# Four branch results turned by VectorE and device memory instead of by TensorE

## The reference

```
h = x @ w_in                                   # 2048 -> 18688 columns, split
y_a = pool_mixer(a_in, ...)      * silu(a_gate)     # each y: 256 tokens x 1024
y_b = spatial_gating(u, v, ...)  * silu(b_gate)
y_c = sliding_window_attention(q, k, v, ...) * silu(c_gate)
y_d = conformer_conv(d_in, ...)  * silu(d_gate)
gates = sigmoid(g_logits)                      # 4 x 2048 columns
merged = sum_i gates[i] * (y_i @ w_branch[i])  # 1024 -> 2048
out = merged @ w_out
x = layer_norm(ALPHA * x + out)
```

## Time and profile before

| | |
|---|---|
| median of three runs | 2425.29 us (2425.19 to 2425.72) |
| profiled execution | 2426.32 us, its span 2424.6 us |
| PE (matmul) busy | 2402.5 us, 99% |
| weight loads of PE busy | 1977.9 us, 82% |
| DVE busy | 1800.6 us, 74% |
| ACT busy | 1119.0 us, 46% |
| POOL busy | 162.2 us, 7% |
| TensorE clock granted | 0.999 of full |
| moved by DMA | 556.93 MB, mean 230 GB/s |

### The profile page before, as it was taken

The page is one execution under the profiler, slowest core; times in us unless marked ns, Lnnn a source line. Parts: engine busy times, 40 slices in busy tenths (PEclk is TensorE's granted clock), DMA queues, the critical chain, the costliest instruction groups (busy, mean ns, idle before and its releaser), DMA issues.

```text
span 2424.6 us, 28710 instructions
## 1 busy us (share of the span) xinstructions
PE 2402.5 (99%) x11098; PEld 1977.9 (82%) x11098; DVE 1800.6 (74%) x2429; ACT 1119.0 (46%) x1464; POOL 162.2 (7%) x186
## 2 busy tenths in 40 slices
PE   9999999999999999999999999999999999999998
PEld 7888888888888888888788888777788888888887
DVE  5688868888899888788878857677777765555555
ACT  5344444444455454456743333644544443444443
POOL 2010000000000001000011100002000100000000
PEclk9999999999999999999999999999999999999999
DMA  9888766666588668877985656455898976667663
GB/s 303 256 269 273 239 218 195 195 184 195 188 267 267 211 213 292 293 257 255 316 270 186 222 171 233 132 159 177 268 302 283 292 233 193 195 211 227 210 213 124
DMA packets 280100, 556.93 MB, mean 230 GB/s; under 512 B 18503, under 2 KB 23901, under 8 KB 278428
## 3 DMA queue, kind: packets, MB, share of 16 engines
q1 hardware_dynamic: 270588, 515.16, 66.0%
q0 software_dynamic: 9088, 37.85, 5.4%
q10 hardware_dynamic: 288, 2.10, 0.2%
HBM read 543.07 MB, written 15.11 MB: 230 GB/s over the span
## 4 chain that ended last, share of the span: by engine, by line
PE 94%; DVE 3%; issue 1%; ACT 1%; DMA 1%; SPq 0%; POOL 0%; ACTq 0%; POOLq 0%; DVEq 0%
PE pb L2155 92%; PE pb L2159 3%; DVE wlo L1395 1%; DMA raw<-in_w_in 1%; DVE acc L1417 1%; ACT whi L939 0%; DVE sm L1946 0%; DVE x L1774 0%; DVE across L1427 0%; DVE gn L2015 0%; DVE x L1777 0%; DVE x L1495 0%; DVE stz L1497 0%; DVE x L1510 0%; DVE fl L2003 0%
## 5 line engine op out<-in xcount | busy, mean ns | idle before, releaser
L939 ACT ACTIVATE whi<-raw 128x1024 fp32r<-128x1024 f32 (+1 forms) x791 | 828.2, 1049 | 1105.5 <-PE pb L2155 1030.5
L1395 DVE TENSOR_TENSOR wlo<-raw,whi 128x1024 fp32r<-128x1024 f32 (+1 forms) x791 | 958.1, 1218 | 446.8 <-ACT whi L939 444.6
L2155 PE MATMUL pb<-whi,xh 128*128 128x512 f32 (+1 forms) x1184 | 465.1, 393 | 0.7 <-DVE xl L1548 0.7
L2155 PE MATMUL pb<-whi,xl 128*128 128x512 f32 (+1 forms) x1184 | 458.2, 387 | 0.0
L2155 PE MATMUL pb<-wlo,xh 128*128 128x512 f32 (+1 forms) x1184 | 457.6, 386 | 0.0
L1417 DVE SCALAR_TENSOR_TENSOR acc<-raw,silc,acc 128x512 f32<-128x512 f32 x480 | 346.1, 752 | 5.7 <-DMA raw<-in_w_ada 0.7
L2155 PE MATMUL pb<-whi,fh 128*128 128x512 f32 x704 | 274.8, 390 | 1.4 <-DVE fl L2003 1.4
L2155 PE MATMUL pb<-whi,fl 128*128 128x512 f32 x704 | 274.0, 389 | 0.0
L2155 PE MATMUL pb<-wlo,fh 128*128 128x512 f32 x704 | 273.9, 389 | 0.0
L2155 PEld LDWEIGHTS pb<-whi,xh 128*128 128x128 f32 x1184 | 222.6, 188 | 46.6 <-issue 2.9
L2155 PEld LDWEIGHTS pb<-whi,xl 128*128 128x128 f32 x1184 | 222.3, 188 | 46.0
(11 more groups left out here) (426 smaller groups left out, 2828.9 us busy)
## 6 DMA issues: line engine op xcount, KB each, us to landing
raw<-in_w_in SPq DMA_DIRECT2D x375, 512.0 KB, 4.6
raw<-in_w_ada SPq DMA_DIRECT2D x192, 512.0 KB, 4.9
raw<-in_ffn_wg SPq DMA_DIRECT2D x88, 512.0 KB, 4.4
raw<-in_ffn_wu SPq DMA_DIRECT2D x88, 512.0 KB, 4.8
raw<-in_ffn_wd SPq DMA_DIRECT2D x88, 512.0 KB, 4.1
raw<-in_w_branch SPq DMA_DIRECT2D x64, 512.0 KB, 3.9
raw<-in_w_out SPq DMA_DIRECT2D x64, 512.0 KB, 4.4
scr_h<-sil POOLq DMA_DIRECT2D x11, 512.0 KB, 4.0
```

The source lines that it names most:

```text
L939: return eng.activation(dst, src, ACT.Copy)
L1395: tt(wlo[:, u, a:b, 0:n], raw[:, l % NRAW, a:b, 0:n], f32(whi[:, u, a:b, 0:n]), ALU.subtract) \
L2155: return eng.matmul(dst, l, r, start=start, stop=stop)
```

## The change

PE's `rows_T` and its four chains are taken out. In its place, for each branch c:

- DVE (`turn`): two `transpose` instructions of 128x1024, one for each block of tokens, which turn each 32x32 block in place within its 32 partitions, into the new tile `yt`. Beats: A 38, B 100, D 258, C 309.
- POOL (`branches`): one beat later, when both are done, one DMA of 1 MB from `yt` to the new tensor `scr_y[c]`; two beats after that it waits for its landing and issues four gathers of 256 KB into `ys`, one for each quarter of the partitions. `yt` and `ys` are the same memory (`oS1`, 8 KB a partition).
- ACT (`branch_high`) and DVE (`branch_low`): the same four pieces of `yh` and `yl` as before, now read from `ys` in SBUF with a turned order of columns, after all four gathers. Beats on both engines: A 44 to 47, B 177 to 180, D 265 to 268, C 317 to 320.
- The waits of other chains for `yT` become waits for `turned`, the loads for x again count from a beat of their own, `B["res"]` (which leaves them where they stood), and the loading of `lnr` and the second attention buffer, which share `oS1`, wait for `yl`.

The diff, cut to its core:

```diff
+def by_rows(ap):
+    return ap.rearrange("p k (t r) -> p t k r", t=8)
...
+        scr_y = {c: dram(f"scr_y{c}", [2, 128, 1024]) for c in "ABCD"}
+        yt = at("yt", oS1, [128, 2, 1024])
+        ys = at("ys", oS1, [128, 8, 8, 32])
...
-        B["yA"] = [E["a_gt1"] + 7 + f for f in range(4)]
+        B["turn"] = {"A": E["a_gt1"] + 7, "B": E["dv1"] + 5}
+        B["yA"] = [E["a_gt1"] + 12 + f for f in range(4)]
...
-        B["yD"] = [B["swish"][3] + 4 + f for f in range(4)]
+        B["turn"]["D"] = B["swish"][3] + 3
+        B["yD"] = [B["turn"]["D"] + 6 + f for f in range(4)]
-        B["yC"] = [E["bD3"] + 1 + f for f in range(4)]
+        B["turn"]["C"] = B["heads"][3] + 10
+        B["yC"] = [B["turn"]["C"] + 7 + f for f in range(4)]
+        B["res"] = E["bD3"] + 4
...
             def attention1():
-                yield from until(B["yD"][3] + 1)
-                W.wait_ge("yT", "D", 3)
+                yield from until(B["turn"]["D"] + 4)
+                W.wait_ge("turned", "D", 1)
...
+            def branches(c):
+                yield from until(B["turn"][c] + 1)
+                W.wait_ge("turned", c, 1)
+                eng.dma_start(scr_y[c].rearrange("t p x -> p t x"), yt[:, :, :]) \
+                    .then_inc(*M.inc(S("scr_y"), "scr_y", c, by=16))
+                yield from until(B["turn"][c] + 3)
+                W.wait_ge("scr_y", c)
+                rows = scr_y[c].rearrange("t (i c) x -> c (t i) x", i=4)
+                for a in range(4):
+                    eng.dma_start(ys[32 * a:32 * a + 32, :, :, :].rearrange("p t k r -> p t (k r)"),
+                                  rows[:, :, 256 * a:256 * a + 256]) \
+                        .then_inc(*M.inc(S("ys_in"), "ys", c, a, by=16))
...
+            def branch_high(c, b, *free):
+                for kp in range(4):
+                    yield from until(b[kp] + 1)
+                    if kp == 0:
+                        for k in free:
+                            W.wait_ge(*k)
+                    W.wait_ge("ys", c, 3)
+                    copy(by_rows(yh[:, 2 * kp:2 * kp + 2, :]), ys[:, :, 2 * kp:2 * kp + 2, :]) \
+                        .then_inc(*M.inc(S("branch_hi"), "yh", c, kp))
...
+            def turn(c, src, *ready):
+                yield from until(B["turn"][c])
+                for e in ready:
+                    W.wait_ge(*e)
+                for tb in XT:
+                    eng.transpose(yt[:, tb, :].rearrange("p (a k r) -> p a k r", a=4, k=8),
+                                  src[:, tb, :].rearrange("p (k a c) -> p a k c", k=8, a=4)) \
+                        .then_inc(*M.inc(S("branch_t"), "turned", c, tb))
+
+            def branch_low(c, b):
+                for kp in range(4):
+                    yield from until(b[kp] + 1)
+                    W.wait_ge("yh", c, kp)
+                    tt(by_rows(yl[:, 2 * kp:2 * kp + 2, :]), ys[:, :, 2 * kp:2 * kp + 2, :],
+                       by_rows(f32(yh[:, 2 * kp:2 * kp + 2, :])), ALU.subtract) \
+                        .then_inc(*M.inc(S("branch_lo"), "yl", c, kp))
...
-            def rows_T(key, b, src, freed, *ready):
-                for kp in range(len(b)):
-                    yield from until(b[kp])
-                    ps = take((*key, kp), (*freed, kp), b[kp] + 1)
...
-                            ins = tr(ps[:, (2 * k + tb) * 128:(2 * k + tb + 1) * 128], src[:, tb, kt * 128:(kt + 1) * 128])
-                    ins.then_inc(*M.inc(S("side"), *key, kp))
```

More of the change, by code:

```diff
@@ L382, in program @@
         for s in range(2):
-            win(f"dv{s}", 7424 + 512 * s, 512, ("copy", half(d_n, s), (("yT", "A", 3),)))
+            win(f"dv{s}", 7424 + 512 * s, 512, ("copy", half(d_n, s), (("turned", "A", 1),)))
         for s in range(2):
@@ L780, in residual @@
                 for k in range(4):
-                    yield from until(B["yC"][3] + 2 + 6 * k)
-                    W.wait_ge("yT", "C", 3)
+                    yield from until(B["res"] + 2 + 6 * k)
+                    W.wait_ge("turned", "C", 1)
                     ks = slice(512 * k, 512 * k + 512)
@@ L785, in residual @@
                 for i, n in enumerate(("ln_g", "ln_b")):
-                    yield from until(B["yC"][3] + 26 + 6 * i)
+                    yield from until(B["res"] + 26 + 6 * i)
+                    W.wait_ge("yl", "C", 3)
                     eng.dma_start(lnr[i][:, :], I[n][0].partition_broadcast(128)) \
@@ L791, in context @@
                 for tb in range(2):
-                    yield from until(B["yC"][3] + 38 if tb == 0 else B["hc"][0] + 13)
+                    yield from until(B["res"] + 38 if tb == 0 else B["hc"][0] + 13)
                     if tb == 0:
@@ L919, in pool @@
             chains = [start(), na_table(), band_table(), ln_rows("ln_b", B["ln_b"], 1, "sgu_ln_g", "sgu_ln_b"),
-                      ln_rows("ln_d", B["ln_d"], 3, "conv_ln_g", "conv_ln_b"), tables(), attention1(), residual(), fold(),
+                      ln_rows("ln_d", B["ln_d"], 3, "conv_ln_g", "conv_ln_b"), tables(), *[branches(c) for c in "ABDC"],
+                      attention1(), residual(), fold(),
                       context(), norm1(), gqa(), mla1(), out2(), gates(), norm2(), hidden(), final(), na_bias(), diff()]
@@ L959, in evacuate @@
                     W.wait_ge("acc", s.name, tb)
-                    W.wait_ge("yT", "B", 3)
+                    W.wait_ge("turned", "B", 1)
                     k = ps[:, 0:128].rearrange("p (k d) -> p k d", k=2)
@@ L1462, in evacuate @@
                     if s.name[:2] == "ds":
-                        W.wait_ge("yT", "A", 3)
+                        W.wait_ge("turned", "A", 1)
                         W.wait_ge("grp", 3)
                     elif s.name[:2] == "cg":
-                        W.wait_ge("yT", "B", 3)
+                        W.wait_ge("turned", "B", 1)
                     ev(tt(s.evac[1](tb), g, ps, ALU.mult))
@@ L1691, in heads1 @@
                         else:
-                            W.wait_ge("yT", "D", 3)
-                            W.wait_ge("swTp", 1)
+                            W.wait_ge("turned", "D", 1)
+                            if u:
+                                W.wait_ge("yl", "D", 3)
                         p = side("lg1", g, hp, i)
@@ L2065, in hidden @@
                     kt = 4 * s % 24
[L2066 to L2067 removed]
+                    tt(by_rows(idl[:, kt:kt + 4, :]), hs[:, :, :, :],
+                       by_rows(f32(idh[:, kt:kt + 4, :])), ALU.subtract) \
                         .then_inc(*M.inc(S("hidden_lo"), "idl", s, 0))
@@ L2098, in dve @@
                 xT(kp)
-            chains = [small_start(), mixer(), low(("yh", "A"), ("yl", "A"), B["yA"], yh, yl, ("yT", "A")),
+            chains = [small_start(), mixer(), turn("A", a_in, ("swTp", 1), ("grp", 3)), branch_low("A", B["yA"]),
                       norm_rows("ln_b", B["ln_b"], 1, lambda tb: v_n[:, tb, :], ("ea", "v1", 1)), sgu(),
-                      low(("yh", "B"), ("yl", "B"), B["yB"], yh, yl, ("yT", "B")), conv(),
+                      turn("B", u_n, ("yl", "A", 3), ("sgu_out", 3)), branch_low("B", B["yB"]), conv(),
                       norm_rows("ln_d", B["ln_d"], 3, lambda tb: d_y[:, tb, :], ("dyc", 3)),
-                      low(("yh", "D"), ("yl", "D"), B["yD"], yh, yl, ("yT", "D")),
+                      turn("D", d_y, ("yl", "B", 3), ("y_d", 3)), branch_low("D", B["yD"]),
                       *[heads1(g) for g in range(4)],
-                      low(("yh", "C"), ("yl", "C"), B["yC"], yh, yl, ("yT", "C")),
+                      turn("C", c_g, ("out1", 2), ("out1", 3)), branch_low("C", B["yC"]),
                       low(("mh",), ("ml",), B["mT"], mh, ml, ("mT",)), tables(), context(), norm1(),
@@ L2505, in pe @@
             mlw = (("Tc", "mkn", 3), ("Tc", "mqr", 3), ("Tc", "mqn", 3), ("kpT",))
[L2506 to L2509, removed]
+            chains = [small_start(), mixer(), sgu(), conv(), qk1(), *[heads1(g) for g in range(4)], merged_T(),
                       *[scaled_T("hc", [B["hc"][tb] + 5 + k for k in range(8)], (tb,), "hct", lambda t: ctn, (0,),
```

10 lines of the change are left out of this document (5 added, 5 removed).

## The result

The changed kernel takes **2446.82 us**, median of 4 runs (2444.76 to 2449.63), against 2425.24 for the kernel before on the same chip: a ratio of 1.0089, 95% interval 1.0074 to 1.0104. It is slower by 21.6 us, where 2425.7 was forecast and the range ended at 2431.

A forecast was written before the change was run, and what follows sets the result against it. PE, busy in every microsecond from 30 to 1110 us, was taken as the bound. -7.7 (transposes off PE) + 5.1 (A) + 3.0 (D) = +0.4 us gave 2425.7 us, range 2417.5 to 2431.

The forecast's parts named there:

- Taken off PE, -7.7: On PE, sixteen groups of four transposes removed, 0.48 us each: -7.7 us, 1.9 a branch.
- DVE: On DVE, two block transposes more and cheaper remainders: net 2.2 to 2.8 us a branch, hidden by cover at B and C.
- The transfers: On POOL's queue, per branch a 1 MB write of 6 to 7 us, then 9 to 10 to the last gather.
- A, +5.1: Branch A: gathers landed at 155.5, wlo late at beat 48, then short until beat 57: +5.1 us, bounds 0 and 9.3.
- D, +3.0: Branch D: 2 MB more delay weights, making the first four heads' softmax late: +3.0 us, bounds 0 and 6.4.
- C, 0: Branch C: gathers landed at 922.5, before ACT reaches beat 317 at 923.8: 0 us, bounds 0 and 2.
- The first: Rival: transfers at A and D are hidden anyway, only the -7.7 left, 2417.6 us; chance 0.28.
- The second: Rival: DMA bandwidth at D, beats 269 to 276, becomes the bound; 6 at D, 8.4 at A, 2432.0 us; chance 0.17.
- The third: Rival: PE can't use the gap of removed transposes, gain nil at D and C, -3.9, 2421.4 us; chance 0.05.

The follow-up runs named there:

- e2: Changed kernel with the band table's 3 MB DMA moved from before branch A's write to beat 71, after its gathers; 2441.03 us, ratio 1.0060.
- e1: Changed kernel with only branch A's rounding twenty beats later (beats 64 to 67), turning and transfers unmoved; 2435.3 us, ratio 1.0037.
- e3: Kernel before, without the change, plus eight useless DVE instructions at beat 44, 10.06 us together; 2436.23 us, ratio 1.0040.
- e13: Changed kernel, all four branches, A's rounding late, PE's transposes of folded sums two beats later at D and C, x loads later; 2425.38 us, ratio 0.9997.
- e6: Kernel before plus D's and C's write and gathers, whose result nobody uses; 2426.04 us, ratio 1.0001.
- e10: e1 with branch D alone turned by PE again; 2429.47 us, ratio 1.0015.
- e14: e10 with PE's transposes of the folded sums two beats later at C alone, x loads unmoved; 2423.19 us, ratio 0.9988.
- e11: e10 with PE's transposes of the folded sums two beats later at C alone and the x loads six beats later; 2422.26 us, ratio 0.9983.
- e8: e1 with branch D's rounding six beats later too; 2440.03 us, ratio 1.0057.
- e7: e1 with branches D and C turned by PE as before, only A and B by DVE; 2424.62 us, ratio 0.9995.
- e9: e7 with the band table's 3 MB written later, at beat 71; 2425.74 us, ratio 0.9998.
- e4: Changed kernel with PE's transposes of folded sums two beats later everywhere; 2440.9 us, ratio 1.0060.

## Why the prediction was wrong

*Taken off PE, -7.7.* Right: sixteen steps of 0.47 to 0.50, 7.7 us together.

*DVE.* Two block transposes take 2.36 us, not 2.75; yl from SBUF takes 684 ns, not 611. The net of 2.3 is within its bounds.

*The transfers.* Mis-sized: 8.7 us from the write's landing to the last gather, bound 12. Measured from the first issue it is 13.5 at A (147.7 to 161.2), 12.3 at B, 13.0 at D, 10.8 at C, and 12.4 in e2 with the queue to themselves. I took the middle between two values from half-size gathers. (The fit of the Trainium skill, "DMA: Bandwidth & Descriptors", section on the anatomy of one DMA on the gpsimd path, which the prediction cites, 4.4 us for such a write, is under all writes here: 5.4 to 14.1.) What this was worth at A: by the prediction's own rule, a microsecond of PE for each of lateness, 161.2 in place of 155.5 would have made 5.1 to 10.8, and 6.6 of the 17.4 would be left. And e2 says that the landing isn't the whole: with all on land by 152.7, where the rule gives 2.3, A still loses 8.5.

*A, +5.1 against 17.4.* The failed step is what DVE's lateness costs PE: the wlo of beat 48 and then a shortage of wlo at beat 57, and nothing else. The first wait was that wlo, as forecast, but 5.7 long instead of 0.6, from the late gathers. The second was not wlo. I followed what stands behind the waiting DVE instruction to wlo and stopped. The same beat held the end of an `ada` pair, whose way leads through POOL to a PE instruction of fixed place, with 3.4 us of cover where I counted on 8.1. That wait is 6.8 us (the fold took 7.4 next to DVE's catching up), and with 5.7 for wlo and 4.7 for the half clock, which the sum had at nothing, it makes 17.2. e1 and e3 show the step, from both sides. The shortage itself is real but small: with A's rounding late and the table where it was, PE waits 0.9 to 1.3 us at beat 57 in all seven kernels.

*D, +3.0 against 7.3.* That the weights come late was right, and so was the softmax, as second in line (e13: 1.6 us). First in line were the sums again. Pricing the transfers by their bandwidth (2 MB more, 6.4 us, half of it taken) is refuted by e6, and PE's lead alone costs nothing in e10; it takes both together.

*C, 0 against 5.4.* The failed step is the same, an omitted chain. The bounds of 0 and 2 looked at the gathers alone, and ACT did not wait for them. But their bytes delayed the weights (5.4 us at 946.2), and behind these stood the third pair with 3.6 us of cover. e10 and e14 show it.

*Rivals.* The first needed 8 us of cover, which only wlo had. The second named a cause, bandwidth at D, that alone costs nothing. The third is refuted by the steps at every branch. None was the mechanism.

*What remains at A with the rounding late* (1.2 to 5.3 us between kernels with the same A) follows the weights. ACT waits for those of one beat, beside the gathers, until 157.1, 157.5 and 157.6 us in e10, e11 and e14, and PE has no wait at beat 49; until 158.8 and 158.9 in e8 and e1, and PE waits 0.5 and 1.0; until 160.2 and 160.7 in e13 and e7, and it waits 1.7 and 2.1. In e9, without the table ahead of them, it is over at 152.0.

*Still open.* How D could be saved, and what makes the weights come earlier in one execution than in another. That DVE's two-input instructions stretch the fold is read off the traces, with and without them beside it; no kernel was run that changes only this.

## What to carry to other kernels

For each instruction that will wait, list all that stands behind it on its engine to the end of the beat, and follow each item through the other engines to the first one that the bound engine needs. The least of these covers counts, less the time by which the bound engine now arrives earlier; a cover measured at one product says nothing of the others. Place the consumer of a transfer as late as its own user allows, and when a wait appears look first whether a small group in the bound engine's order can move by a beat or two: four transposes moved by two beats were worth some 6 us at C, the sixteen groups removed 7.7. At D the same move gave 2 us or less (e4, e13), since the weights were late behind it.

## What the runs showed of the hardware

- A POOL `tensor_tensor` of 128x512 took 1.29 us with DVE idle and 7.38 beside seven DVE subtractions from SBUF; it ended 1.1 to 1.2 us after the run did.
- A wait of PE of 5.7 or 6.8 us was followed by 3.6 and 5.7 us of work at granted clock 0.50. One of 4.3 at D was followed by the lower level too. One of 3.8 at C was followed by the full clock in the changed kernel and by the lower one in e1 and e10 (until 948.8 and 942.6), so the length of the wait alone doesn't settle it.
- Four gathers of 256 KB each, from a 1 MB tensor written just before, took 12.4 us alone on their queue at A (e2), the write 5.4. While such gathers move, ACT waited 7.1 to 8.6 us for one slice of weights (e1, e7, e8, e10, e11, e13, e14), a wait that the kernel before doesn't have there.
